# First two attentions of a two-block network: scaled negative queries, a minimum in the mask, rope on GpSimd, and an earlier copy

## The chip, the cores and the metric

The kernel runs on one core of a Trainium2 chip. What is measured is the device time of one execution, in microseconds; a run is one timed execution, and times are given as the median of several.

A core has five engines with queues of their own: TensorE (PE, matrix products and transposes, written to PSUM), VectorE (DVE), ScalarE (ACT), GpSimd (POOL), and SyncE (SP), which here only issues DMAs. Engines meet in semaphores: an instruction adds one to a semaphore when it is done, and another engine waits in its own queue until the count is there. An engine executes its queue strictly in order.

## The reference, cut to what matters

One batch of 256 tokens with model width 1024 goes through a first block and then two layers of a second one, all in fp32. The change lies wholly in the first block's mixer, which has two attentions over the same 256 tokens:

```python
h = rms_norm(x, mix_norm_g[layer])
proj = h @ w_in[layer]
q_a, k_a, v_a, c_q, c_kv, k_pe, gate_a, gate_b = jnp.split(proj, splits, axis=-1)
q_a = apply_rope(q_a.reshape(B, S, A_HEADS, A_HEAD_DIM), cos_a, sin_a)      # 8 heads of 64
k_a = apply_rope(k_a.reshape(B, S, A_HEADS, A_HEAD_DIM), cos_a, sin_a)
y_a = moba_attention(q_a, k_a, v_a)     # one block of 256 keys: plain causal attention here
# second attention (MLA), 8 heads of 64 + 32 with rope on the 32:
q = (rms_norm(c_q, q_norm_g) @ w_q_up).reshape(B, S, B_HEADS, B_NOPE + B_ROPE)
kv = (rms_norm(c_kv, kv_norm_g) @ w_kv_up).reshape(B, S, B_HEADS, B_NOPE + B_V)
# q_pe, k_pe: apply_rope; k_pe is shared by the heads
# both attentions, per head:
s = q @ k.T * scale ; s = where(k_pos <= q_pos, s, -inf) ; p = softmax(s) ; y = p @ v
merged = sigmoid(gate_a) * (y_a @ w_branch_a) + sigmoid(gate_b) * (y_b @ w_branch_b)
x = x + merged @ w_out[layer]
```

Here `apply_rope` gives, for the halves x1 and x2, `x1*cos - x2*sin` and `x2*cos + x1*sin`. Then come a product-key expert layer (128 x 128 experts, all computed densely in the kernel) and the second block.

## The kernel before, in words

All weights come as a stream of 128-row chunks of up to 1024 columns, in one fixed order (`chunk_plan`). The four-deep ring `w_raw` takes them. Each chunk j passes four hands: SP loads it (once the split of chunk j-4 is complete), ACT writes its rounded part w_hi (`split`, L1345; needs the load, and PE done with chunk j-4), POOL writes the rest w_lo = w_raw - w_hi (`rest`, L1863), and PE multiplies three products for each block (hi·hi, lo·hi, hi·lo; L625 to L627 for row groups, L818 to L820 in `gate_b`). ACT and POOL do this three chunks ahead of PE. Their other work is written by hand between these steps: ACT's `split_to(n)` runs the splits up to chunk n-1, and POOL's main loop has calls ahead of `rest(j)` for chosen j.

The order of groups in the stage that matters: qk (8 chunks), vc (8), ga (8), qup (2), kvup (1), gb (8), br_a (4), br_b (4), wout (8). In ga, PE also transposes the rotated queries and keys of the first attention (`a_maps`, ahead of chunk ga+2) and the normalised low-rank rows (`c_maps`, ahead of ga+6). ACT copies the former to QTA (L1423). ACT computes the sigmoid of gate a from the finished banks (L1381, `evacuate("ga", ...)`), and PE starts qup only when these banks are free.

Then one loop over 16 heads u runs: 0 to 7 are the first attention's, 8 to 15 the second's. For each, PE does in this order: `causal_fills(u)`, the three transposes of the probabilities (L756, waits for exponential u; for heads 5 to 12 it waits also for `qb_E`, since the PSUM bank mb is used by the b_map too, and for heads 13 and 14 for `yA_E`); `scores(u+2)` (L747, L748); `head_values(u-1)` (L762 to L764); for u from 4 to 11 `b_map(u)` (L789), the transposes of two heads of QB (even u) or KF (odd u); for u 12 and 13 `y_map` (L799), transposes of the first attention's result; and `gate_b(u)`, one sixteenth of the gate b product, two heads to a chunk, which is spread over the heads so that PE has work while the softmax is computed. `gate_b(0)` writes banks 2 and 3, and waits for `kv_act`: kvup's second half was there.

DVE does per head `masked` (L2198): scores plus mask out of PSUM to Sm with the row maximum (a custom instruction and an accumulator read for each half), and then L2203, which multiplies the 128x2 maxima by -scale, for the bias of the exponential. Behind it in the same iteration stands head-specific work: for u = 1 the first half of KF and VB (L2228, L2229), for u = 2 to 6 the rope of the second attention (L2238 to L2257: six instructions for the queries QB in place, six for the keys, two that copy the rotated keys into KF for all heads), for u = 10 the normalisation `branch_out(0)` (L2208, L2211), for u = 6 to 13 the copy of the transposed heads to QTB (L2264), for u = 14 and 15 the low part of yA (L2269).

ACT does per head the two exponentials with accumulated sums (L1453, L1455), then `copy_probs(u-1)` (L1435), then special work: at u = 1 the splits of gb+1 and gb+2, the copies of token half 1 of KF and VB (L1465, L1466) out of banks 2 and 3, which signal `kv_act`, and the split of gb+3; at odd u from 3 a split; at u = 8 the copy of gate b's first half (L1444); at u = 12 and 13 the high part of yA (L1477).

Of the kernel before, what the change touches and what calls it, by code (L numbers as in the profile page):

```python
# [194 lines left out]
def share(semaphore, signals):  # L195
# [33 lines left out]
    **share("small_dve", [("angles", 1), ("rope_a", 1), ("cn", 1), ("cT", 3), ("rope_q", 1),  # L229
                          ("rope_k", 1), ("rope_b", 2), ("y", 4), ("best", 1), ("picks", 1),  # L230
# [3 lines left out]
    **share("small_pool", [("l2_r", 1), ("vb", 1), ("zg", 1), ("v_mean", 1), ("kd", 1), ("v_r", 1),  # L234
# [6 lines left out]
def program(nc, ins, out):  # L241
    ctx = ExitStack()
    with ctx:
# [1084 lines left out]
        def _(act):  # L1328
# [118 lines left out]
            for u in range(A_H + B_H):  # L1447
                scale = (A_DH if u < A_H else B_DK) ** -0.5
                act.wait_ge(sem("masked"), u + 1)
                if u >= 2:  # L1450

                    act.wait_ge(sem("pT"), upto("pT", u - 1))
                f(Pr[:, u % 2, 0:P], Sm[:, u % 2, 0:P], ACT.Exp, bias=mx[:, u, 0:1], scale=scale,  # L1453
                  accum_out=sums[:, u, 0:1]).then_inc(sem("exp0"), 1)
                f(Pr[:, u % 2, P:3 * P], Sm[:, u % 2, P:3 * P], ACT.Exp, bias=mx[:, u, 1:2],  # L1455
                  scale=scale, accum_out=sums[:, u, 1:2]).then_inc(sem("exp"), 1)
                if u:
                    copy_probs(u, PT, "pT", "pv", u - 1, "pT_E")
                if u == 1:

                    split_to(FIRST["gb"] + 3)
                    for n in range(2):
# [367 lines left out]
        def _(pool):  # L1830
# [35 lines left out]
            def block_masks():  # L1866
# [6 lines left out]
                causal_mask(causal1)  # L1873
# [170 lines left out]
        def _(dve):  # L2044
# [172 lines left out]
            for u in range(A_H + B_H):  # L2217
                dve.wait_ge(sem("scores"), u + 1)
                if u >= 2:

                    dve.wait_ge(sem("exp"), u - 1)
                masked(Sm[:, u % 2, :], col[u % 2], causal, mx[:, u, :],
                       (A_DH if u < A_H else B_DK) ** -0.5, "masked")
# [7 lines left out]
                if u == 2:  # L2231
                    cos, sin = (over(ang[:, :, ph, 32:48], [P, NT, 8, 16], 2) for ph in (1, 0))
                    q1, q2 = QB[:, :, :, 64:80], QB[:, :, :, 80:96]
                    k1, k2 = VC[:, :, 896:912], VC[:, :, 912:928]
                    rq = [rope_t[:, :, 8 * a:8 * a + 8, 16 * b:16 * b + 16] for a in range(2)
                          for b in range(2)]
                    rk = [rope_u[:, :, a, 0:16] for a in range(6)]
                    go(v.tensor_tensor(rq[0], q1, cos, ALU.mult))  # L2238
                    go(v.tensor_tensor(rq[1], q2, sin, ALU.mult))
                if u == 3:  # L2240
                    go(v.tensor_tensor(rq[2], q2, cos, ALU.mult))
                    then(v.tensor_tensor(rq[3], q1, sin, ALU.mult))
                if u == 4:
                    go(v.tensor_tensor(q1, rq[0], rq[1], ALU.subtract))
                    then(v.tensor_tensor(q2, rq[2], rq[3], ALU.add), "rope_q")
                if u == 5:
                    kc, ks = ang[:, :, 1, 32:48], ang[:, :, 0, 32:48]
                    go(v.tensor_tensor(rk[0], k1, kc, ALU.mult))
                    go(v.tensor_tensor(rk[1], k2, ks, ALU.mult))
                    go(v.tensor_tensor(rk[2], k2, kc, ALU.mult))  # L2250
                    then(v.tensor_tensor(rk[3], k1, ks, ALU.mult))
                    go(v.tensor_tensor(rk[4], rk[0], rk[1], ALU.subtract))
                    then(v.tensor_tensor(rk[5], rk[2], rk[3], ALU.add), "rope_k")
                if u == 6:
                    dve.wait_ge(sem("dve"), counts["dve"])
                    for n in range(2):
                        then(v.tensor_copy(KF[:, :, :, 64 + 16 * n:80 + 16 * n],  # L2257
                                           over(rk[4 + n], [P, NT, 8, 16], 2)), "rope_b")
# [669 lines left out]
```

## Time and profile before

| what | value |
|---|---|
| three runs | 1779.05, 1779.22, 1781.5 us; median 1779.22 |
| the profiled execution, its time | 1778.86 us |
| its span (first to last instruction) | 1777.1 us |
| mean granted TensorE clock | 0.992 of full |
| busy: PE / ACT / DVE / POOL | 97% / 52% / 51% / 58% |
| HBM read | 285.01 MB, 162 GB/s mean over the span |

Time and span differ by 1.8 us outside the instructions. The profile comes from one execution. Its views are used here as follows: the first part gives each engine's share; the list of waits says who waited for whom; the timeline gives one engine's instructions in order with the idle time before each; windows give each engine's busy time and the granted clock in a stretch (1.00 is 2.4 GHz, 0.50 is 1.2 GHz). An idle time in brackets names the engine and line whose signal ended it, by the latest signal found. The ends of PE's matmuls are modelled.

### The profile page before, as it was taken

How to read it: one execution, taken by the hardware profiler on the slowest of the kernel's cores; microseconds unless marked ns; L12 is line 12 of the kernel's file. 1: busy time of each engine (PE TensorE's matmuls, PEld its weight loads, DVE VectorE, ACT ScalarE, POOL GpSimd, SP SyncE). 2: the span in 40 equal slices, each digit the busy share in tenths (PEclk: the TensorE clock that was granted, in tenths of full speed). 3: DMA queues.
4: the chain of work that ended last, by engine and by line, in shares of the span. 5: the costliest groups of instructions: out<-in, count | busy, mean ns of one | idle time of the engine just before them, and what ended most of it. 6: DMA issues, size and time to landing. Idle time of an engine off the chain costs nothing.

```text
span 1777.1 us, 32153 instructions
## 1 busy us (share of the span) xinstructions
PE 1728.1 (97%) x10852; PEld 1549.5 (87%) x10852; DVE 905.0 (51%) x1838; ACT 925.3 (52%) x1596; POOL 1037.8 (58%) x542
## 2 busy tenths in 40 slices
PE   8989999999999999999999999899999999999998
PEld 6778899999999999888888888888999877789997
DVE  6563329990777776555555547743111266521112
ACT  5555556676333334544544556625554566555544
POOL 7835768888666665000000057716888886588886
PEclk9999999999999999999999999999999999999999
DMA  6523555555444444555555555104555555255553
GB/s 205 173 91 111 174 183 178 178 182 186 152 138 139 141 143 162 193 191 196 192 191 195 197 181 175 64 25 139 187 188 186 177 171 165 69 188 187 188 185 123
DMA packets 83074, 288.23 MB, mean 162 GB/s; under 512 B 9264, under 2 KB 9264, under 8 KB 82480
## 3 DMA queue, kind: packets, MB, share of 16 engines
q1 hardware_dynamic: 82560, 286.10, 49.1%
q10 hardware_dynamic: 432, 1.05, 0.2%
q8 instruction: 50, 0.82, 0.2%
q14 instruction: 32, 0.26, 0.0%
HBM read 285.01 MB, written 2.10 MB: 162 GB/s over the span
## 4 chain that ended last, share of the span: by engine, by line
PE 90%; ACT 3%; DVE 3%; POOL 2%; issue 2%; DMA 0%; DVEq 0%; ACTq 0%; POOLq 0%
PE acc L625 14%; PE acc L626 14%; PE acc L627 14%; PE col L662 12%; PE col L663 12%; PE col L664 12%; PE mb L923 3%; POOL w_lo L1863 1%; PE acc L1074 1%; PE mb L697 1%; ACT hT_hi L1369 1%; ACT w_hi L1345 1%; PE acc L1197 0%; PE mb L904 0%; PE col L1074 0%
## 5 line engine op out<-in xcount | busy, mean ns | idle before, releaser
L1863 POOL TENSOR_TENSOR w_lo<-w_raw,w_hi 128x1024 fp32r<-128x1024 f32 (+1 forms) x410 | 975.6, 2400 | 351.3 <-ACT w_hi L1345 350.8
L1345 ACT ACTIVATE w_hi<-w_raw 128x1024 fp32r<-128x1024 f32 (+1 forms) x539 | 565.3, 1052 | 350.9 <-PE acc L627 305.4
L662 PE MATMUL col<-hT_hi,w_hi 128*128 128x256 f32 x1632 | 468.1, 287 | 2.1 <-DVE hT_lo L2080 1.5
L664 PE MATMUL col<-hT_hi,w_lo 128*128 128x256 f32 x1632 | 461.9, 283 | 0.0
L663 PE MATMUL col<-hT_lo,w_hi 128*128 128x256 f32 x1632 | 461.8, 283 | 0.0
L662 PEld LDWEIGHTS col<-hT_hi,w_hi 128*128 128x128 f32 x1632 | 312.7, 192 | 5.1 <-issue 1.9
L663 PEld LDWEIGHTS col<-hT_lo,w_hi 128*128 128x128 f32 x1632 | 312.9, 192 | 2.3
L664 PEld LDWEIGHTS col<-hT_hi,w_lo 128*128 128x128 f32 x1632 | 312.6, 192 | 0.0
L625 PE MATMUL acc<-w_hi,W_hi 128*128 128x512 f32 x512 | 199.3, 389 | 0.0
L626 PE MATMUL acc<-w_lo,W_hi 128*128 128x512 f32 x512 | 199.3, 389 | 0.0
L627 PE MATMUL acc<-w_hi,W_lo 128*128 128x512 f32 x512 | 199.3, 389 | 0.0
L1905 POOL TENSOR_SCALAR_AFFINE_SELECT WST<-WST 128x512 f32<-128x512 f32 x1 | 0.6, 635 | 320.3 <-DMA WST<-in_gmlp_w 320.3
L2687 DVE CAST H_hi<-mb 128x256 fp32r<-128x256 f32 x64 | 27.2, 424 | 289.4 <-ACT mb L1717 289.4
L2449 DVE TENSOR_TENSOR w_lo<-w_raw,w_hi 128x1024 fp32r<-128x1024 f32 x128 | 156.2, 1221 | 0.7 <-ACT w_hi L1345 0.6
L625 PE MATMUL acc<-w_hi,hT_hi 128*128 128x512 f32 x368 | 144.8, 394 | 9.0 <-POOL w_lo L1863 3.5
L626 PE MATMUL acc<-w_lo,hT_hi 128*128 128x512 f32 x368 | 142.6, 388 | 0.0
L627 PE MATMUL acc<-w_hi,hT_lo 128*128 128x512 f32 x368 | 142.0, 387 | 0.0
L2427 DVE TENSOR_TENSOR W_lo<-act_e,W_hi 128x256 fp32r<-128x256 f32 x128 | 54.5, 426 | 147.3 <-ACT W_hi L1554 146.7
L627 PEld LDWEIGHTS acc<-w_hi,W_lo 128*128 128x128 f32 x512 | 96.1, 188 | 20.0
L626 PEld LDWEIGHTS acc<-w_lo,W_hi 128*128 128x128 f32 x512 | 96.1, 188 | 19.9
L625 PEld LDWEIGHTS acc<-w_hi,W_hi 128*128 128x128 f32 x512 | 96.1, 188 | 19.8
L625 PE MATMUL acc<-w_hi,H_hi 128*128 128x512 f32 x256 | 100.4, 392 | 0.0
(543 smaller groups left out, 2681.6 us busy)
## 6 DMA issues: line engine op xcount, KB each, us to landing
w_raw<-in_expert_u SPq DMA_DIRECT2D x128, 512.0 KB, 3.5
w_raw<-in_expert_v SPq DMA_DIRECT2D x128, 512.0 KB, 3.5
w_raw<-in_w_mlp SPq DMA_DIRECT2D x128, 512.0 KB, 3.5
w_raw<-in_w_in SPq DMA_DIRECT2D x24, 512.0 KB, 3.7
w_raw<-in_w_qkv_o SPq DMA_DIRECT2D x24, 512.0 KB, 3.8
w_raw<-in_w_query SPq DMA_DIRECT2D x16, 512.0 KB, 3.7
w_raw<-in_w_gate SPq DMA_DIRECT2D x16, 512.0 KB, 3.5
w_raw<-in_w_qkv_e SPq DMA_DIRECT2D x12, 512.0 KB, 3.8
```

The lines of the kernel that those rows point to most:

```text
L625: mm(o, hi(t), w_hi[:, s, a:b], start=first, stop=False)
L626: mm(o, hi(t), w_lo[:, s, a:b], start=False, stop=False)
L627: m = mm(o, lo(t), w_hi[:, s, a:b], start=False, stop=last)
L662: mm(o, wh[:, k, :], hi[:, k, :], start=k == 0, stop=False)
L663: mm(o, wh[:, k, :], lo[:, k, :], start=False, stop=False)
L664: m = mm(o, wl[:, k, :], hi[:, k, :], start=False, stop=k == KD - 1)
L923: m = mm(mb[s % 2][:, t * P:(t + 1) * P], hot2[:, s % 2, t, :], hot1[:, s % 2, t, :], start=True, stop=True)
L1345: f(w_hi[:, s, 0:w], w_raw[:, s, 0:w], ACT.Copy).then_inc(sem(f"hi{s}"), 1)
L1863: g.tensor_tensor(w_lo[:, s, 0:w], w_raw[:, s, 0:w], w_hi[:, s, 0:w].bitcast(F32), ALU.subtract).then_inc(sem(f"lo{s}"), 1)
L2427: v.tensor_tensor(lo[:, q, :], act_e[:, c, :], hi[:, q, :].bitcast(F32), ALU.subtract).then_inc(sem("W_lo"), 1)
L2449: v.tensor_tensor(w_lo[:, s, :], w_raw[:, s, :], w_hi[:, s, :].bitcast(F32), ALU.subtract).then_inc(sem(f"lo{s}"), 1)
L2687: v.tensor_copy(H_hi[:, s, :], H_q[s]).then_inc(sem("H_hi"), 1)
```

## The change

The queries of both attentions carry -scale: ACT's copy of the transposed queries of the first attention to QTA multiplies them by -1/8, and DVE's copy to QTB of the second attention's transposed queries by -96^-0.5. The mask holds +1e30 in place of -1e30 above the diagonal, `masked` takes the minimum instead of the maximum, and the exponential has scale -1 with that minimum as its bias; the multiplication of L2203 falls away. The rope of the second attention moves from DVE to POOL: the keys' before `rest(ga+6)`, the queries' before `rest(gb+1)`. In ACT's iteration u = 1, the copies of KF and VB come right behind the exponentials, ahead of `copy_probs(0)` and ahead of the splits of gb+1 to gb+3.

```diff
@@ ACT
                 f(QTA[:, 2 * b:2 * b + 2, :].rearrange("p a s -> p (a s)"), mb[b % 2][:, :],
-                  ACT.Copy).then_inc(sem("qa_E"), 1)
+                  ACT.Copy, scale=-A_DH ** -0.5 if b < 2 else 1.0).then_inc(sem("qa_E"), 1)
...
             for u in range(A_H + B_H):
-                scale = (A_DH if u < A_H else B_DK) ** -0.5
...
-                f(Pr[:, u % 2, 0:P], Sm[:, u % 2, 0:P], ACT.Exp, bias=mx[:, u, 0:1], scale=scale,
+                f(Pr[:, u % 2, 0:P], Sm[:, u % 2, 0:P], ACT.Exp, bias=mx[:, u, 0:1], scale=-1.0,
                   accum_out=sums[:, u, 0:1]).then_inc(sem("exp0"), 1)
...
-                if u:
-                    copy_probs(u, PT, "pT", "pv", u - 1, "pT_E")
                 if u == 1:
-
-                    split_to(FIRST["gb"] + 3)
                     for n in range(2):
                         acc_full(act, "kvup", 2 + n)
                         kv = acc[2 + n][:, :].rearrange("p (h d) -> p h d", h=4)
                         f(KF[:, 1, 4 * n:4 * n + 4, 0:B_NOPE], kv[:, :, 0:B_NOPE], ACT.Copy)
                         f(VB[:, 1, 4 * n:4 * n + 4, :], kv[:, :, B_NOPE:], ACT.Copy).then_inc(
                             sem("kv_act"), 1)
+                if u:
+                    copy_probs(u, PT, "pT", "pv", u - 1, "pT_E")
+                if u == 1:
                     split_to(FIRST["gb"] + 4)
@@ POOL
-            def causal_mask(m):
+            def causal_mask(m, fill):
...
-            causal_mask(causal)
+            causal_mask(causal, -NEG)
...
+            def rotate_key():
+                pool.wait_ge(sem("ev_vc"), upto("ev_vc", 4))
+                pool.wait_ge(sem("rope_a"), upto("rope_a", 1))
+                x1, x2 = VC[:, :, 896:912], VC[:, :, 912:928]
+                rk = [rope_u[:, :, a, 0:16] for a in range(6)]
+                cos, sin = rope_cs()
+                g.tensor_tensor(rk[0], x1, cos, ALU.mult).then_inc(sem("rope_k"), 1)
+                g.tensor_tensor(rk[1], x2, sin, ALU.mult).then_inc(sem("rope_k"), 1)
+                g.tensor_tensor(rk[2], x2, cos, ALU.mult).then_inc(sem("rope_k"), 1)
+                g.tensor_tensor(rk[3], x1, sin, ALU.mult).then_inc(sem("rope_k"), 1)
+                pool.wait_ge(sem("rope_k"), 4)
+                g.tensor_tensor(rk[4], rk[0], rk[1], ALU.subtract).then_inc(sem("rope_k"), 1)
+                g.tensor_tensor(rk[5], rk[2], rk[3], ALU.add).then_inc(sem("rope_k"), 1)
+                pool.wait_ge(sem("rope_k"), 6)
+                for n in range(2):
+                    g.tensor_copy(KF[:, :, :, 64 + 16 * n:80 + 16 * n],
+                                  rk[4 + n].unsqueeze(2).to_broadcast([P, NT, 8, 16])).then_inc(
+                        sem("rope_b"), 1)
+            def rotate_queries():
+                pool.wait_ge(sem("ev_qup"), upto("ev_qup", 4))
+                x1, x2 = QB[:, :, :, 64:80], QB[:, :, :, 80:96]
...
+                g.tensor_tensor(rq[0], x1, cos, ALU.mult).then_inc(sem("rope_p"), 1)
+                g.tensor_tensor(rq[1], x2, sin, ALU.mult).then_inc(sem("rope_p"), 1)
+                g.tensor_tensor(rq[2], x2, cos, ALU.mult).then_inc(sem("rope_p"), 1)
+                g.tensor_tensor(rq[3], x1, sin, ALU.mult).then_inc(sem("rope_p"), 1)
+                pool.wait_ge(sem("rope_p"), 4)
+                g.tensor_tensor(x1, rq[0], rq[1], ALU.subtract).then_inc(sem("rope_p"), 1)
+                pool.wait_ge(sem("rope_p"), 5)
+                g.tensor_tensor(x2, rq[2], rq[3], ALU.add).then_inc(sem("rope_q"), 1)
...
+                if j == FIRST["ga"] + 6:
+                    rotate_key()
+                if j == FIRST["gb"] + 1:
+                    rotate_queries()
@@ DVE
-            def masked(dst, src, mask, top, scale, name):
+            def masked(dst, src, mask, low, name):
                 for t, (a, b) in enumerate(((0, P), (P, 3 * P))):
-                    i = v.tensor_tensor_reduce(dst[:, a:b], src[:, a:b], mask[:, a:b], 1.0, LOWEST,
-                                               ALU.add, ALU.max, top[:, t:t + 1])
-                    if t == 0:
-                        go(i)
-                then(i)
-                then(v.tensor_scalar(top, top, -scale, None, ALU.mult), name)
+                    i = v.tensor_tensor_reduce(dst[:, a:b], src[:, a:b], mask[:, a:b], 1.0, -LOWEST,
+                                               ALU.add, ALU.min, low[:, t:t + 1])
+                i.then_inc(sem(name), 1)
...
-                if u == 2:
-                    (the rope of u = 2 to 6: 12 tensor_tensor and 2 tensor_copy)
...
-                    then(v.tensor_copy(QTB[0:B_DK, 2 * b:2 * b + 2, :].rearrange("p a s -> p (a s)"),
-                                       mb[(u + 1) % 2][0:B_DK, :]), "qb_E")
+                    heads_ = QTB[0:B_DK, 2 * b:2 * b + 2, :].rearrange("p a s -> p (a s)")
+                    turned_ = mb[(u + 1) % 2][0:B_DK, :]
+                    if b < 4:
+                        then(v.tensor_scalar(heads_, turned_, -B_DK ** -0.5, None, ALU.mult), "qb_E")
+                    else:
+                        then(v.tensor_copy(heads_, turned_), "qb_E")
```

## Rows read from the trace of the kernel before

**Rows 1.** The page's first part: busy time, share of the span, instructions, by engine.
```profile
PE 1728.1 (97%) x10852; PEld 1549.5 (87%) x10852; DVE 905.0 (51%) x1838; ACT 925.3 (52%) x1596; POOL 1037.8 (58%) x542
```

**Rows 2.** The list of waits, 50 to 160 us: total us, times, longest.
```profile
PE mb L756 <- ACT Pr L1455: 4.2, 4, 1.9
```

**Rows 3.** Timeline of PE: start, duration, instruction, idle time before it and releaser.
```profile
76.94 0.48 PE L625 MATMUL acc<-w_hi,hT_hi 128*128 128x512 f32 x1
...
95.48 0.50 PE L818 MATMUL acc<-w_hi,hT_hi 128*128 128x512 f32 x1 [2.71 <-ACT VB L1466]
...
100.40 0.49 PE L756 MATMUL mb<-ident,Pr 128*128 128x128 f32 x3
...
102.36 0.48 PE L818 MATMUL acc<-w_hi,hT_hi 128*128 128x512 f32 x1
...
113.19 0.52 PE L756 MATMUL mb<-ident,Pr 128*128 128x128 f32 x3 [1.94 <-ACT Pr L1455]
...
130.19 0.52 PE L756 MATMUL mb<-ident,Pr 128*128 128x128 f32 x3 [1.12 <-ACT Pr L1455]
...
148.85 0.52 PE L756 MATMUL mb<-ident,Pr 128*128 128x128 f32 x3 [0.94 <-ACT Pr L1455]
```

**Rows 4.** Windows: stretch, length, busy of PE, PEld, DVE, ACT, POOL; clock, DMA, GB/s.
```profile
114.40:116.50 2.10, 2.10 (x11) 1.98 (x11) 0.81 (x5) 0.93 (x4) 0.00 (x0) 0.52 0.09 31
116.50:118.00 1.50, 1.50 (x6) 1.23 (x5) 0.69 (x1) 0.06 (x1) 0.00 (x0) 0.53 0.00 0
```

**Rows 5.** Timeline of ACT.
```profile
80.02 1.06 ACT L1345 ACTIVATE w_hi<-w_raw 128x1024 fp32r<-128x1024 f32 x1 [2.55 <-PE acc L627]
...
91.95 0.49 ACT L1435 ACTIVATE PT<-mb 128x384 f32<-128x384 f32 x1 [0.40 <-PE mb L756]
92.34 1.99 ACT L1345 ACTIVATE w_hi<-w_raw 128x1024 fp32r<-128x1024 f32 x2
...
125.00 1.38 ACT L1444 ACTIVATE GB<-acc,rstd 128x512 f32<-128x512 f32 x2 [1.92 <-PE acc L820]
...
147.44 0.50 ACT L1455 ACTIVATE Pr<-Sm,mx 128x256 f32<-128x256 f32 x1
```

**Rows 6.** Timeline of DVE.
```profile
79.16 0.49 DVE L2070 TENSOR_SCALAR cT_hi<-mb,cols 128x256 fp32r<-128x256 f32 x1
...
109.42 2.30 DVE L2203 TENSOR_SCALAR mx<-mx 128x2 f32<-128x2 f32 x1
...
112.40 0.69 DVE L2264 COPY QTB<-mb 96x512 f32<-96x512 f32 x1
...
146.18 1.85 DVE L2203 TENSOR_SCALAR mx<-mx 128x2 f32<-128x2 f32 x1
```

**Rows 7.** One line's instructions: duration in ns min/median/max, first and last start.
```profile
L2203 DVE TENSOR_SCALAR mx<-mx x16: 168/170/2297, 89.5 to 146.2; 128x2 f32<-128x2 f32 x16
```

**Rows 8.** Timeline of POOL.
```profile
67.28 4.78 POOL L1863 TENSOR_TENSOR w_lo<-w_raw,w_hi 128x1024 fp32r<-128x1024 f32 x2 [0.31 <-ACT w_hi L1345]
...
77.55 1.85 POOL L1863 TENSOR_TENSOR w_lo<-w_raw,w_hi 128x768 fp32r<-128x768 f32 x1 [0.88 <-ACT w_hi L1345]
...
85.84 2.38 POOL L1863 TENSOR_TENSOR w_lo<-w_raw,w_hi 128x1024 fp32r<-128x1024 f32 x1 [2.31 <-ACT w_hi L1345]
93.46 7.22 POOL L1863 TENSOR_TENSOR w_lo<-w_raw,w_hi 128x1024 fp32r<-128x1024 f32 x3 [5.23 <-ACT w_hi L1345]
```

**Rows 9.** Groups by form, DVE: count | busy us, mean ns | idle before.
```profile
L2780 DVE CUSTOM_DVE_ANT_0 S<-col,ALIBI 128x256 f32<-128x256 f32 x16 | 6.7, 419 | 0.0
```

**Rows 10.** Groups by form, POOL.
```profile
L1863 POOL TENSOR_TENSOR w_lo<-w_raw,w_hi 128x1024 fp32r<-128x1024 f32 x395 | 943.1, 2407 | 350.3 <-ACT w_hi L1345 349.9 <-issue 0.2
...
L1917 POOL TENSOR_TENSOR ms<-ss 128x1 f32<-128x1 f32 x18 | 4.6, 253 | 20.7 <-ACT junk L1361 20.7
...
L1899 POOL TENSOR_TENSOR masks<-masks 128x128 f32<-128x128 f32 x1 | 1.3, 1314 | 0.1
```

**Rows 11.** DMA issues, 71 to 77 us: KB each, us from issue to landing.
```profile
w_raw<-in_w_kv_up SPq DMA_DIRECT2D x1, 512.0 KB, 3.4
```

More of the change, by code:

```diff
@@ L228 @@
                           ("lam_exp", 1), ("qk_root", 2), ("o1_ss", 4)]),
[L229 to L230 removed]
+    **share("small_dve", [("angles", 1), ("rope_a", 1), ("cn", 1), ("cT", 3), ("y", 4), ("best", 1), ("picks", 1),
                           ("x_final", 4), ("sp", 2), ("g_ready", 1), ("k_map", 1),
@@ L233 @@
                           ("o1", 4)]),
-    **share("small_pool", [("l2_r", 1), ("vb", 1), ("zg", 1), ("v_mean", 1), ("kd", 1), ("v_r", 1),
+    **share("small_pool", [("rope_b", 2), ("rope_q", 1), ("l2_r", 1), ("vb", 1), ("zg", 1), ("v_mean", 1), ("kd", 1), ("v_r", 1),
                            ("gv", 1), ("dec_q", 1), ("o_r", 2),
@@ L1452, in _ @@
                     act.wait_ge(sem("pT"), upto("pT", u - 1))
-                f(Pr[:, u % 2, 0:P], Sm[:, u % 2, 0:P], ACT.Exp, bias=mx[:, u, 0:1], scale=scale,
+                f(Pr[:, u % 2, 0:P], Sm[:, u % 2, 0:P], ACT.Exp, bias=mx[:, u, 0:1], scale=-1.0,
                   accum_out=sums[:, u, 0:1]).then_inc(sem("exp0"), 1)
                 f(Pr[:, u % 2, P:3 * P], Sm[:, u % 2, P:3 * P], ACT.Exp, bias=mx[:, u, 1:2],
-                  scale=scale, accum_out=sums[:, u, 1:2]).then_inc(sem("exp"), 1)
-                if u:
-                    copy_probs(u, PT, "pT", "pv", u - 1, "pT_E")
+                  scale=-1.0, accum_out=sums[:, u, 1:2]).then_inc(sem("exp"), 1)
                 if u == 1:
-                    split_to(FIRST["gb"] + 3)
                     for n in range(2):
@@ L1848, in causal_mask @@
                     d = m[:, c * P:(c + 1) * P]
-                    then(g.affine_select(out=d, in_=d, compare_op=ALU.is_ge, fill=NEG, base=0,
+                    then(g.affine_select(out=d, in_=d, compare_op=ALU.is_ge, fill=fill, base=0,
                                          pattern=[[-1, P]], channel_multiplier=1), "causal")
-            causal_mask(causal)
+            causal_mask(causal, -NEG)
             g.iota(iota_row[:, :], [[1, P]], base=0, channel_multiplier=0,
@@ L1871, in block_masks @@
                 used(pool, V0 + 1)
-                causal_mask(causal1)
+                causal_mask(causal1, NEG)
                 for c, base in ((0, 0), (1, P), (2, 0)):
@@ L1921, in row_rstd, with rope_cs @@
                 norms[0] += 1
+            def rope_cs(heads_=None):
+                cs = [ang[:, :, ph, 32:48] for ph in (1, 0)]
+                return cs if heads_ is None else [c.unsqueeze(2).to_broadcast([P, NT, heads_, 16])
+                                                  for c in cs]
+            def rotate_key():
[16 more added lines that the diff above has]
+                        sem("rope_b"), 1)
@@ new lines, in rotate_queries @@
+            def rotate_queries():
+                pool.wait_ge(sem("ev_qup"), upto("ev_qup", 4))
+                x1, x2 = QB[:, :, :, 64:80], QB[:, :, :, 80:96]
+                rq = [rope_t[:, :, 8 * a:8 * a + 8, 16 * b:16 * b + 16] for a in range(2)
+                      for b in range(2)]
+                cos, sin = rope_cs(8)
+                g.tensor_tensor(rq[0], x1, cos, ALU.mult).then_inc(sem("rope_p"), 1)
[6 more added lines that the diff above has]
+                g.tensor_tensor(x2, rq[2], rq[3], ALU.add).then_inc(sem("rope_q"), 1)
@@ L2221, in _ @@
                     dve.wait_ge(sem("exp"), u - 1)
-                masked(Sm[:, u % 2, :], col[u % 2], causal, mx[:, u, :],
-                       (A_DH if u < A_H else B_DK) ** -0.5, "masked")
+                masked(Sm[:, u % 2, :], col[u % 2], causal, mx[:, u, :], "masked")
                 if u == 1:
@@ L2230, in _ @@
                              "ev_kvup")
-                if u == 2:
[L2232 to L2258, printed above, removed]
                 if u == A_H + 2:
```

## The prediction, made before the changed kernel was run

> **What bounds the kernel now.** First the page's first part: TensorE (PE) is busy for 97% of the span, so only time in which PE waits, or runs at the lower clock, can be won [rows 1]. The changed code runs between 57 and 155 us. There the list of waits has one wait of PE that comes four times, on the exponentials of L1455, 4.2 us in all [rows 2]. PE's own timeline shows where PE is idle: 2.71 us before 95.48, 1.94 before 113.19, 1.12 before 130.19, 0.94 before 148.85 (the fourth wait on L1455 is the small rest, before 144.26) [rows 3]. Between them PE works back to back: from the first gate step (95.48) to the third (102.36) two heads pass in 6.88 us, 3.44 a head. Last the windows: from 114.4 to 118.0 us, behind the wait of 1.94, the granted clock was 0.52 and 0.53, so nearly all at the lower level (1.2 GHz) [rows 4].
>
> A wait for several semaphores is put down to the last one that the profile names, so each needs its real cause.
> - Before 95.48 PE stands at the first gate step, which waits for `kv_act`, ACT's copies of KF and VB out of banks 2 and 3. ACT was done with the second exponential at 91.55 (91.95 less 0.40 idle), copied head 0's transposes, ran two splits (92.34 to 94.33), and only then those copies [rows 5]. PE had been ready at 92.77.
> - Before 113.19 the transposes of head 5 also wait for `qb_E`, the copy to QTB. It ended at 113.09, and stands in DVE's order behind the KF copies and L2203, a tensor_scalar on 128x2 numbers that took 2.30 us here [rows 6], where its median is 0.17 [rows 7]. All its operands lie in SBUF, and POOL was in a w_lo subtraction, as it was in three of them from 93.46 on, 2.41 us each [rows 8]: DVE stood until POOL's instruction was over.
> - Before 130.19 it is again that copy, this time behind the normalisation of the first attention, which stays.
> - Before 148.85 it is `yA_E`: the subtraction of L2269 stood behind another held L2203, from 146.18 to 148.03 [rows 6].
>
> **The change part by part.** The sum is made against the profiled execution, 1778.86 us, of which 1777.1 are span. The median of the runs, 1779.22, lies 0.36 above it.
>
> 1. *KF and VB ahead of the splits.* ACT can begin at 91.55. Before, the four copies lay between 94.33 and PE's start at 95.48, so they take 1.1; `kv_act` comes at 92.7 and PE is ready at 92.77. The wait of 2.71 goes. What is late next: copy_probs(0), 0.49, and three splits of 0.99 now stand behind the copies [rows 5], to 96.2, and exponential 2 behind them, about 0.9 long, to 97.1. PE reaches the transposes of head 2 4.92 us behind the first gate step (95.48 to 100.40), now at 97.7. Cover 0.6 us. Bounds -2.7, and -1.6 if exponential and copies both come 1.2 late. I take **-2.7**, since each duration is one of this stage.
> 2. *L2203 gone, the mask as a minimum.* The 16 instructions leave DVE, not PE's path. The minimum form runs already in the last attention, 419 ns for 128x256 [rows 9], as the maximum does here: no cost. In head 6 nothing stands before the QTB copy any more. It starts when PE's transposes are there and fits inside the gate step that follows them (3.44 less 1.96, the time from 100.40 to 102.36: 1.48): 0.69 for the plain copy, and scaled between 0.69 and 0.98 (twice the 0.49 of a tensor_scalar out of PSUM on 128x256 [rows 6]); I take 0.75. The wait goes: **-1.9**. So does what lay behind it: 2.10 x 0.48 + 1.50 x 0.47 = 1.7 us lost at half clock [rows 4]. Bounds 0, if the clock falls elsewhere, and -1.7; **-1.7**, as no such gap is left ahead of it.
> 3. *The wait before 130.19* shrinks by L2203's 0.17 and grows by the 0.06 of the scaled copy: **-0.1**.
> 4. *The wait before 148.85.* The subtraction then waits only for ACT's yA_hi, and the exponential of head 14 decides, whose last part ended at 148.0 (147.44 and 0.50) [rows 5]: **-0.8**, bounds 0 and -0.94.
> 5. *The scale in QTA.* The nearest ACT row with a scale, out of PSUM at 128x512, is 0.69 each (125.00) [rows 5], about 0.1 over the plain copy. Bounds 0 and +0.2, as two copies are scaled; I take 0: that scale was a tensor, this is a constant.
> 6. *rotate_key on POOL*, ahead of the subtraction of chunk ga+6: six instructions of 128x32, two of 128x256. POOL's rows are 253 ns at one element and 2407 at 1024 [rows 10], so 2.1 ns an element: 6 x 0.32 + 2 x 0.79 = 3.5 us. From below 8 x 0.253 = 2.0; from above 8 x 1.314 = 10.5, by the slowest such row (128x128). That subtraction is the second of the pair that ended at 72.06 [rows 8], and PE needs it at 76.94 [rows 3]: cover 4.9 us. SP issues the load of kvup when this subtraction ends; it lands 3.4 us later [rows 11], now at 79.0, and ACT's split of it started at 80.02 [rows 5]: cover 1.0 beyond the 3.5, and POOL is idle again by 77.55. **0**. Above 4.6 us the split is late, with it the sigmoid behind it on ACT, and PE, which waits for the sigmoid ahead of qup.
> 7. *rotate_queries on POOL*, ahead of gb+1: free at 88.22, POOL had nothing until 93.46 [rows 8]. Six of 128x256 at 0.79 and three waits: 5.0 us, to 93.3. From below 6 x 0.253 = 1.5; from above 6 x 2.63 = 15.8, at 1314 ns for each 128 elements. The subtraction of gb+1 follows ACT's split (94.2) and ends at 96.6; PE asks for it at the third gate step, 92.77 + 6.88 = 99.65. So the rotation may take 8.8 us, 1.4 an instruction. **0**.
> 8. *The rope instructions leave DVE.* PE waited for none of them; nothing more.
>
> A rule speaks against parts 6 and 7. POOL's row is 2407 ns for 128x1024 [rows 10], DVE's for 256 elements out of PSUM 0.49 [rows 6]. The Trainium skill, GPSIMD Engine Reference, section 4.1 Engine selection, gives elementwise work with two inputs to VectorE, because GpSimd is roughly 2x slower. By that, an estimate, the queries' six would take 2 x 0.49 each, 5.9 us in place of 5.0. Either lies inside the 8.8, so the sum would be the same; what the rule prices is the engine's time, not the path.
>
> Another bears on the scaled QTB copy. The tensor_scalar out of PSUM at 79.16 took 0.49 us [rows 6] beside a subtraction on POOL (77.55 to 79.40) [rows 8]: not held. The Trainium skill, SBUF — State Buffer, section Who interferes with whom, names tensor_scalar among the operations that may take the port pair that VectorE shares with GpSimd, given their operands. If it did here, each of the four scaled copies could cost up to 2.4; the row says it does not.
>
> Sum: 2.7 + 1.9 + 1.7 + 0.1 + 0.8 = 7.2. The later stages start on PE's work and on loads that PE's progress sets free, so it is carried to the end. 1778.86 - 7.2 = 1771.7 for an execution like the profiled one, and 1779.2 - 7.2 = 1772.0 for the median.
>
> **The rivals.**
> - *A new wait at heads 2 and 3.* ACT's queue is now copies, copy_probs, three splits, exponential; 1 us more in it and PE waits at head 2, and the clock may fall behind that gap. For it: a cover of only 0.6. Against: no step of ACT got longer. It takes 1.2 of part 1 and the 1.7 of the clock: 1774.9.
> - *The wait before 113.19 stays*, because something else than QTB held it. For it: the profile names the exponential. Against: that one too stood behind L2203, and 113.09 fits 113.19. Then 1.9 and 1.7 are missing: 1775.6.
> - *GpSimd is slow on small, strided, broadcast operands* (the other side). At the 1314 ns row's rate rotate_key takes 10.5, and PE waits for ga+6 until 69.7 + 10.5 + 2.4 = 82.6 instead of 76.94: +5.7. rotate_queries ends at 104.2 and gb+1 at 106.6 instead of 99.65: +7.0. The clock adds 1.7 at least. -7.2 + 14.4 = +7.2: 1786.4. It costs from 1.3 times my price on (the 4.6 of part 6) and from 1.8 times in part 7; at 2.2 times the two cost 3.1 and 2.2 and the clock 1.7, about what the change gains: slower from there. Against: it is one row, the two others give a sixth of it for one element and half of it an element for many.
> - *Nothing measurable*: GpSimd at 1.7 to 2.1 times my price, or a later stage that waits on something not set free by PE: 1777.
>
> **How the numbers follow.** A difference under 0.2%, 3.6 us, can't be told from none for this kernel. Forecast 0.70; new wait 0.11; the wait stays 0.06; nothing measurable 0.09; slow GpSimd 0.04. Over 3.6 us faster: the forecast, and 0.13 of the first two rivals' 0.17: 0.83. Within: 0.13. Slower: 0.04. The forecast's own range is 1770.3 to 1773.7. The range goes down by 2.4 for a clock that also stays up elsewhere, and up over the first two rivals: 1769.6 to 1775.8.
>
> **What would show it.** Right: the first gate step at about 92.8 with no idle before it; none before head 5's transposes, and a granted clock of 1.00 from 92 to 128; about 1 us of idle left before head 9's and 0.15 before head 14's transposes; POOL's rope at 69.7 to 73.2 and 88.4 to 93.4, each instruction under 0.9 us. Wrong: any of them over 1.4 us, PE waiting for w_lo at ga+6 or the third gate step, a longer wait ahead of qup, or a stretch at the lower clock before 155.

## The result: 10 to 12 us faster, where 7.2 were forecast

| kernel | median us (executions) | range | ratio to before, 95% interval |
|---|---|---|---|
| before, first comparison | 1780.36 (4) | 1779.05 to 1783.83 | |
| changed, first comparison | 1770.11 (4) | 1769.12 to 1771.48 | 0.9938 (0.9919 to 0.9958) |
| before, second comparison | 1781.48 (23) | 1776.79 to 1787.78 | |
| changed, second comparison | 1769.75 (6) | 1769.06 to 1770.98 | 0.9931 (0.9915 to 0.9948) |

The change is faster, as forecast, but by 0.6 to 0.7% instead of 0.4%. The medians themselves, 1770.11 and 1769.75, lie inside the range of 1769.6 to 1775.8 us. As ratios to 1779.22 that range is 0.9946 to 0.9981, and both measured ratios lie below it. The difference is in the kernel before, which is slower than its first three runs showed (1779.22): its executions spread over 11 us, those of the changed kernel over 2.4. The two profiled executions, by contrast, differ by what was forecast: spans 1777.1 and 1769.7, 7.4 us.

The experiments below were timed in three groups, each with the kernel before beside it: medians 1781.48 (23 executions), 1781.53 (20) and 1781.17 (23). Ratios are to the kernel before of the same group. The changed kernel was timed again only in the first, so a difference from it can be one between groups. One execution of rope_on_dve, 2125.17 us at a mean clock of 0.751 where its others had 0.994 to 0.995, is left out.

PE's timeline of the changed kernel (L755 is the old L756, L817 the old L818, L624 the old L625):

```profile
92.77 0.50 PE L817 MATMUL acc<-w_hi,hT_hi 128*128 128x512 f32 x1
...
97.69 0.49 PE L755 MATMUL mb<-ident,Pr 128*128 128x128 f32 x3
...
99.65 0.48 PE L817 MATMUL acc<-w_hi,hT_hi 128*128 128x512 f32 x1
...
108.36 0.49 PE L755 MATMUL mb<-ident,Pr 128*128 128x128 f32 x3
...
123.38 0.52 PE L755 MATMUL mb<-ident,Pr 128*128 128x128 f32 x3 [0.77 <-ACT Pr L1454]
...
141.28 0.55 PE L755 MATMUL mb<-ident,Pr 128*128 128x128 f32 x3 [0.17 <-ACT Pr L1454]
...
147.19 0.47 PE L624 MATMUL acc<-w_hi,yA_hi 128*128 128x512 f32 x1 [0.21 <-issue]
```

Held against [rows 3]: the first gate step has no idle time before it, nor have head 2's transposes (97.69) nor head 5's (108.36). 1.12 us before head 9's became 0.77, 0.94 before head 14's 0.17. The stage ends, with the start of br_a, at 147.19 instead of 154.63.

The clock in the stretch in which it had fallen before [rows 4], a window of the changed kernel (length; busy PE, PEld, DVE, ACT, POOL; clock; DMA; GB/s):

```profile
92.00:128.00 36.00, 35.23 (x215) 28.83 (x215) 12.11 (x49) 23.12 (x63) 17.41 (x9) 1.00 0.35 103
```

ACT, to hold against [rows 5]: copies first, then copy_probs, then three splits, and exponential 2 from 95.61 to 96.50, so done 1.2 us before PE needs it at 97.69:

```profile
91.34 0.36 ACT L1460 ACTIVATE KF<-acc 128x256 f32<-128x256 f32 x1
...
92.13 0.37 ACT L1461 ACTIVATE VB<-acc 128x256 f32<-128x256 f32 x1
92.40 0.49 ACT L1435 ACTIVATE PT<-mb 128x384 f32<-128x384 f32 x1
92.77 2.96 ACT L1344 ACTIVATE w_hi<-w_raw 128x1024 fp32r<-128x1024 f32 x3
95.61 0.40 ACT L1452 ACTIVATE Pr<-Sm,mx 128x128 f32<-128x128 f32 x1
...
95.99 0.51 ACT L1454 ACTIVATE Pr<-Sm,mx 128x256 f32<-128x256 f32 x1
```

POOL, to hold against [rows 8]. A 128x32 product starts every 0.21 us, a 128x256 one every 0.70, and the two copies take 0.75 together. The last line is a subtraction during which DVE makes the copy shown next:

```profile
69.75 0.25 POOL L1934 TENSOR_TENSOR rope_u<-VC,ang 128x32 f32<-128x32 f32 x1
...
71.24 0.75 POOL L1943 COPY KF<-rope_u 128x256 f32<-128x256 f32 x2
...
88.53 0.73 POOL L1954 TENSOR_TENSOR rope_t<-QB,ang 128x256 f32<-128x256 f32 x1 [0.21 <-DVE QB L2154]
...
92.25 0.73 POOL L1961 TENSOR_TENSOR QB<-rope_t 128x256 f32<-128x256 f32 x1
93.91 9.38 POOL L1861 TENSOR_TENSOR w_lo<-w_raw,w_hi 128x1024 fp32r<-128x1024 f32 x4 [0.93 <-ACT w_hi L1344]
...
106.60 2.39 POOL L1861 TENSOR_TENSOR w_lo<-w_raw,w_hi 128x1024 fp32r<-128x1024 f32 x1 [3.31 <-ACT w_hi L1344]
```

DVE in head 6, to hold against [rows 6]; the scaled copy lasts as long as the plain one (0.69), although POOL's subtraction of 106.60 to 108.99 runs beside it:

```profile
107.18 0.69 DVE L2279 TENSOR_SCALAR QTB<-mb 96x512 f32<-96x512 f32 x1 [0.60 <-PE mb L788]
```

### The profile page after: what moved, and what is told of

It is laid out like the page before. It is cut to its first block, busy times and chain, and to the rows that moved or that the text cites. A ratio compares the mean times of both kernels' runs of the same rounds, so it can differ in the third digit from the quotient of the medians.

```text
span 1769.7 us, 32125 instructions
## 1 busy us (share of the span) xinstructions
PE 1726.9 (98%) x10852; PEld 1548.3 (87%) x10852; DVE 888.5 (50%) x1808; ACT 925.4 (52%) x1596; POOL 1044.8 (59%) x556
## 4 chain that ended last, share of the span: by engine, by line
PE 90%; ACT 3%; DVE 3%; POOL 2%; issue 1%; DMA 0%; DVEq 0%; ACTq 0%; POOLq 0%
PE acc L624 14%; PE acc L625 14%; PE acc L626 14%; PE col L661 12%; PE col L662 12%; PE col L663 12%; PE mb L922 3%; POOL w_lo L1861 1%; PE acc L1073 1%; PE mb L696 1%; ACT hT_hi L1368 1%; PE col L1073 0%; ACT w_hi L1344 0%; PE acc L1196 0%; PE mb L903 0%
## 5 line engine op out<-in xcount | busy, mean ns | idle before, releaser
L624 PE MATMUL acc<-w_hi,W_hi 128*128 128x512 f32 x512 | 199.2, 389 | 0.0
L625 PE MATMUL acc<-w_lo,W_hi 128*128 128x512 f32 x512 | 199.2, 389 | 0.0
L624 PE MATMUL acc<-w_hi,hT_hi 128*128 128x512 f32 x368 | 144.9, 394 | 8.9 <-POOL w_lo L1861 3.6
L625 PE MATMUL acc<-w_lo,hT_hi 128*128 128x512 f32 x368 | 142.6, 387 | 0.0
L624 PEld LDWEIGHTS acc<-w_hi,W_hi 128*128 128x128 f32 x512 | 96.1, 188 | 20.0
L625 PEld LDWEIGHTS acc<-w_lo,W_hi 128*128 128x128 f32 x512 | 96.1, 188 | 19.9
L624 PE MATMUL acc<-w_hi,H_hi 128*128 128x512 f32 x256 | 100.4, 392 | 0.0
```

The lines of the kernel that those rows point to most:

```text
L624: mm(o, hi(t), w_hi[:, s, a:b], start=first, stop=False)
L625: mm(o, hi(t), w_lo[:, s, a:b], start=False, stop=False)
```

## The experiments

**Where the 11 us are: the stage or outside it.** The changed kernel again, and two more profiled executions of the kernel before, unchanged, called a and b here.

> The changed kernel once more. Every stage boundary of its trace lies 7.4 to 7.5 us ahead of the kernel before, from the start of br_a (147.19 instead of 154.63) to the end. Theory A, the change gives exactly its stage's 7.4 us: ratio 0.9958, difference of medians 7 to 8. Theory B, something outside the stage gives 3 us more: ratio 0.9938 again, about 11. Under A the larger difference came from executions of the kernel before in which the stretches at the lower TensorE clock (1186, 1206, 1504 and 1528 us) lasted longer.

> One more look at the kernel before. If its time is over 1781, clock theory: its trace has a stretch at the lower clock right behind the first gate step (94 to 105 us), which the profiled execution of 1778.86 us had not; if its time is under 1779, none. Rival: the excess lies in the stretches around 1186, 1206, 1504 and 1528 us.

> The same once more, for a second execution: over 1781 with the clock low behind the first gate step, or under 1779 without. Rival as for the first.

after_again gave 1769.75 us. The size is that of theory B (11.7 us by the medians, ratio 0.9931), its place is not: the table below shows nothing outside the stage that would give it. Executions a and b took 1784.06 and 1779.71 us. The first agrees with the forecast. The second had no fall behind the first gate step either, but lies between the two bounds that I had set (1779 and 1781). PE's timeline of execution a:

```profile
95.42 0.80 PE L818 MATMUL acc<-w_hi,hT_hi 128*128 128x512 f32 x1 [2.71 <-ACT VB L1466]
...
117.46 0.52 PE L756 MATMUL mb<-ident,Pr 128*128 128x128 f32 x3 [1.95 <-ACT Pr L1455]
...
129.28 0.52 PE L756 MATMUL mb<-ident,Pr 128*128 128x128 f32 x3 [1.21 <-issue]
...
161.87 0.47 PE L625 MATMUL acc<-w_hi,yA_hi 128*128 128x512 f32 x1 [0.21 <-issue]
```

and its windows:

```profile
88.00:94.00 6.00, 4.70 (x27) 3.25 (x23) 4.76 (x20) 3.98 (x11) 0.80 (x2) 1.00 0.29 87
94.00:96.00 2.00, 0.58 (x1) 0.50 (x2) 1.97 (x2) 2.00 (x6) 2.00 (x2) 0.66 0.00 0
96.00:104.00 8.00, 8.00 (x24) 6.00 (x23) 6.34 (x9) 2.65 (x10) 4.58 (x2) 0.50 0.71 197
104.00:106.00 2.00, 2.00 (x10) 1.22 (x8) 0.00 (x0) 0.78 (x2) 0.00 (x0) 0.78 0.00 0
...
117.00:119.00 2.00, 1.54 (x8) 0.91 (x8) 0.36 (x1) 0.49 (x2) 0.00 (x0) 0.89 0.74 260
119.00:125.00 6.00, 6.00 (x22) 5.28 (x23) 1.50 (x6) 1.44 (x6) 0.00 (x0) 0.50 0.01 3
```

The clock fell towards the end of the 2.71 us wait (1.00 before 94, 0.66 from 94 to 96) and stayed at the lower level until about 105 (L818 takes 0.80 instead of 0.50), and again behind the wait of 1.95 for longer than in the first trace. There is also a new wait, 1.21 before head 7's transposes. DVE's timeline shows why: with PE later, masked(8) and the next subtraction on POOL (126.06 to 128.44) meet, and L2203 is held there too:

```profile
126.46 2.00 DVE L2203 TENSOR_SCALAR mx<-mx 128x2 f32<-128x2 f32 x1
128.49 0.69 DVE L2264 COPY QTB<-mb 96x512 f32<-96x512 f32 x1
```

Execution b had only the second fall, again longer, and the same new wait (1.09 before 124.87, with L2203 held for 1.89 from 122.16):

```profile
113.00:115.00 2.00, 1.83 (x10) 1.33 (x10) 0.37 (x4) 0.49 (x1) 0.00 (x0) 0.84 0.66 229
115.00:121.00 6.00, 6.00 (x22) 5.19 (x22) 1.20 (x4) 1.86 (x6) 0.00 (x0) 0.50 0.00 0
```

Every profiled execution, split at the start of br_a (first PE instruction that reads yA_hi):

| profiled execution | span | stage's end | rest |
|---|---|---|---|
| before, first | 1777.1 | 154.63 | 1622.5 |
| before, b | 1778.0 | 157.45 | 1620.6 |
| before, a | 1782.3 | 161.87 | 1620.4 |
| changed | 1769.7 | 147.19 | 1622.5 |
| changed again | 1767.9 | 147.13 | 1620.8 |
| without_kv | 1773.0 | 150.09 | 1622.9 |
| kv_only | 1773.0 | 151.22 | 1621.8 |
| min_only | 1774.3 | 153.31 | 1621.0 |
| rope_only | 1779.1 | 158.39 | 1620.7 |
| pe_filled | 1778.8 | 157.60 | 1621.2 |
| rope_on_dve | 1769.9 | 146.99 | 1622.9 |
| two_more | 1768.2 | 145.95 | 1622.3 |
| slow_key | 1772.4 | 151.16 | 1621.2 |
| slow_queries | 1776.9 | 155.91 | 1621.0 |

The rest varies by 2.5 us whatever the kernel (the later stretches at the lower clock, around 1180, 1200, 1500 and 1525 us, are longer or shorter). The kernel before reaches the end of this stage at three times that lie 7.2 us apart, the changed kernel in both traces at the same to 0.06. So in the executions that were traced the difference is made in the stage, and the rival, the later stretches, isn't what made execution a slow. Executions of over 1784.06 us were not traced.

The mean clock of every execution says that the spread is one of the clock, though not in which stretch: of the 23 of the kernel before in the second comparison, the five at 0.994 took 1776.8 to 1778.6 us, the five at 0.989 or 0.990 took 1785.2 to 1787.8. A mean clock lower by 0.005 over 1777 us is 8.9 us. The ten of the changed kernel had 0.994 to 0.996.

**ACT's order alone, and the change without it.** kv_only is the kernel before with the u == 1 lines of ACT as changed; without_kv the changed kernel with the old ones:

```diff
-                if u:
-                    copy_probs(u, PT, "pT", "pv", u - 1, "pT_E")
                 if u == 1:
-                    split_to(FIRST["gb"] + 3)
                     (the copies of KF and VB)
+                if u:
+                    copy_probs(u, PT, "pT", "pv", u - 1, "pT_E")
+                if u == 1:
                     split_to(FIRST["gb"] + 4)
```

> The kernel before with only the copies of KF and VB ahead of copy_probs and the splits. Mine: the first gate step starts at 92.8 instead of 95.48 and the wait ahead of head 5's transposes stays near 1.9 us, so -2.8 us. Rival (ACT's order only moves the wait): PE waits at heads 2 to 4 instead, under -1.5. The clock falls behind the wait at head 5 as before, or not; then 1.7 more.

> The changed kernel with ACT's old order in head 1 (splits of gb+1 and gb+2 ahead of the copies of KF and VB). The wait of 2.7 us before the first gate step comes back. Clock theory: behind that wait the granted clock falls to the lower level in part of the executions, for about 11 us as in the trace with the rope alone moved (94 to 105), and that costs up to 5.5 us; so the median is 6 to 9 us over the changed kernel's, and the times spread over 5 us or more. Rival, the wait costs only its length: +2.8, times within 2 us of each other as those of the changed kernel are, and the rest of the 11 us lies elsewhere.

kv_only: 1773.57 us (1771.75 to 1774.77), ratio 0.9949 (0.9932 to 0.9966): 7.9 us by the medians, where 2.8 were forecast and the wait it removes is 2.7 long. without_kv: 1775.71 us (1772.41 to 1778.67), ratio 0.9974 (0.9963 to 0.9984), 6.0 over the changed kernel, with a spread of 6.3: the low end of what the clock theory gave, and twice the rival's 2.8. In its own profiled execution the wait was there (2.72 before 95.67) and the clock did not fall behind it; that execution ended the stage 2.9 late. Its slowest two, 1778.6 and 1778.7 us, had a mean clock of 0.991, its fastest 0.995. So this wait costs about 2.8 in one traced execution and 6.0 in the median; that the clock falls right behind it in the slower ones of without_kv is argued from execution a, not traced.

The forecast for kv_only missed the waits as well. Head 5 waited for nothing (the KF copies ran at 108.35, before POOL's subtraction of 108.96), and head 4 had a new wait. Exponential 4 waited for masked(4), which stood on DVE behind two rope products of the queries, 128x256 with both inputs in SBUF. They took 2.57 and 2.58 us instead of 0.42 beside two subtractions on POOL:

```profile
105.94 0.55 PE L756 MATMUL mb<-ident,Pr 128*128 128x128 f32 x3 [1.38 <-ACT Pr L1455]
```
```profile
98.90 2.57 DVE L2240 TENSOR_TENSOR rope_t<-QB,ang 128x256 f32<-128x256 f32 x1
101.40 2.58 DVE L2241 TENSOR_TENSOR rope_t<-QB,ang 128x256 f32<-128x256 f32 x1
```
```profile
98.80 4.89 POOL L1862 TENSOR_TENSOR w_lo<-w_raw,w_hi 128x1024 fp32r<-128x1024 f32 x2
```

The clock fell behind that wait:

```profile
108.00:110.00 2.00, 2.00 (x10) 1.69 (x10) 1.56 (x6) 1.76 (x5) 1.04 (x1) 0.52 0.00 0
110.00:112.00 2.00, 2.00 (x8) 1.44 (x7) 0.00 (x0) 0.08 (x1) 1.34 (x1) 0.62 0.04 8
```

Much of the 7.9 is therefore not the clock behind the first wait. Execution b had no such fall, and still ended the stage 6.2 us later than kv_only: 2.7 for the wait itself, 0.6 for a shorter second wait (1.38 for 1.95), 1.1 for the wait at head 7 that is gone, and 1.7 for a shorter fall (1.7 us lost instead of 3.4). An earlier PE meets POOL's subtractions at other places.

**PE kept busy in that wait.** pe_filled is the kernel before with

```diff
                 if u == 0:
+                    chunk_in(j)
+                    for n in range(11):
+                        mm(mb[1][:, :], hT_hi[:, 0, 0:P], w_hi[:, s, 0:512], start=True, stop=True)
                     pe.wait_ge(sem("kv_act"), 2)
```

> The kernel before, with 11 products of 128x128 by 128x512 (0.23 us each, 2.5 us) put on PE into a bank that is not in use, in the place of the wait before the first gate step. Nothing else changes: that step still starts at 95.5. Clock theory: the granted clock no longer falls behind it, so the slower executions go: median 1778 to 1779, none over 1781. Rival, the spread comes from elsewhere (the later stretches at the lower clock): median 1781.5 and times up to 1787 as before.

1779.76 us (1774.04 to 1783.99), ratio 0.9991 (0.9979 to 1.0004): the forecast was missed. The median lies over its 1778 to 1779, three of twelve executions took over 1781, and the kernel is not told apart from before. The fill did its work in the trace, no idle time is left before the first gate step and the clock was up there. But the wait of head 5 followed, the clock fell behind it from about 114 to 121, and the held L2203 of head 8 (L2206 here) cost head 7 another 1.46:

```profile
112.94 0.52 PE L756 MATMUL mb<-ident,Pr 128*128 128x128 f32 x3 [1.96 <-ACT Pr L1458]
...
125.02 0.52 PE L756 MATMUL mb<-ident,Pr 128*128 128x128 f32 x3 [1.46 <-issue]
```

So the spread does not come from the first wait alone; the fall behind the second and what follows it are part of it. Whether the fill moved the first fall onto the second wait, these runs can't say.

**The rope alone.** rope_only is the kernel before with the POOL functions, their calls and the shares of the semaphores added, and DVE's rope removed.

> The kernel before with only the rope of the second attention on GpSimd; L2203's multiplication, the maximum and ACT's order stay. If L2203, held by POOL, is what holds QTB at head 6: the wait at head 5 stays at about 1.2 (the two KF copies are gone, 0.7 us), the first gate step stays at 95.5: -0.7, and -2.4 if the clock then stays up. If the rope instructions on DVE were the cause: the wait goes, -3.6.

1780.04 us (1775.0 to 1782.31), ratio 0.9985 (0.9972 to 0.9998). Head 5 waited 1.31, as L2203 alone would have it, and the first gate step 2.97; behind both the clock fell. PE's and DVE's timelines:

```profile
95.48 0.79 PE L817 MATMUL acc<-w_hi,hT_hi 128*128 128x512 f32 x1 [2.97 <-ACT VB L1465]
...
116.95 0.52 PE L755 MATMUL mb<-ident,Pr 128*128 128x128 f32 x3 [1.31 <-issue]
```

```profile
113.84 2.30 DVE L2248 TENSOR_SCALAR mx<-mx 128x2 f32<-128x2 f32 x1
116.17 0.69 DVE L2281 COPY QTB<-mb 96x512 f32<-96x512 f32 x1
```

**The minimum alone, and all but the rope.** min_only has scaled queries, the minimum and no L2203, with rope on DVE and ACT's old order; rope_on_dve is the same with ACT's new order.

> The kernel before with only the scaled queries, the minimum and no L2203; rope stays on DVE, ACT's order stays. Theory of the prediction, L2203 is the cause at head 5: the wait goes, with it the clock's fall, and 0.8 at head 14: -4.5. Rival: the KF copies of head 6 also lie wholly in SBUF and are held in L2203's place by the same subtraction on POOL: wait at head 5 stays at 1.8, only head 14's 0.8 and 0.1 at head 9: -0.9.

> The changed kernel with the rope put back on DVE in heads 2 to 6; scaled queries, minimum and ACT's new order stay. If L2203 was the whole cause at head 5, this is as fast as the changed kernel (-7.4 against before). If the KF copies are held in its place, the wait at head 5 returns (1.9) and with it perhaps the clock's fall (1.7): -3.6 to -5.5.

min_only: 1779.44 us (1776.02 to 1784.96), ratio 0.9991 (0.9978 to 1.0005). The rival held: a wait at head 5 stayed (1.57, forecast 1.8), and the kernel can't be told from before. PE at head 5, then DVE and POOL in head 6:

```profile
112.84 0.52 PE L756 MATMUL mb<-ident,Pr 128*128 128x128 f32 x3 [1.57 <-issue]
```

```profile
109.33 2.68 DVE L2253 COPY KF<-rope_u 128x256 f32<-128x256 f32 x2
112.05 0.69 DVE L2263 TENSOR_SCALAR QTB<-mb 96x512 f32<-96x512 f32 x1
```
```profile
109.34 2.52 POOL L1863 TENSOR_TENSOR w_lo<-w_raw,w_hi 128x1024 fp32r<-128x1024 f32 x1 [4.22 <-ACT w_hi L1345]
```

With L2203 gone the KF copies, also wholly in SBUF, are held by the same subtraction, PE waits 1.57, and its clock falls (0.72 mean from 112 to 118). Taking away L2203 without the KF copies, or the KF copies without L2203, leaves most of the wait. Both together, which is without_kv, leave none and are 5.5 us faster than before by the medians, where min_only alone is 2.0 and rope_only alone 1.4.

rope_on_dve: 1770.94 us (1769.37 to 1771.67), ratio 0.9943 (0.9926 to 0.9961), so 1.2 over the changed kernel by the medians. There the KF copies ran at 106.40, unheld in 0.62, because POOL's subtraction came only at 107.27. With ACT's new order the two happen not to meet; my 3.6 to 5.5 was wrong, since I had put POOL where it was before. So once the rest is changed, moving the rope is worth 1.2 us or less in these runs.

**How slow GpSimd may be.** slow_queries adds 16 products of 128x256 into the scratch, slow_key 20 of 128x32:

```diff
                 pool.wait_ge(sem("rope_p"), 4)
+                for n in range(16):
+                    g.tensor_tensor(rq[n % 4], (x1, x2, x2, x1)[n % 4], (cos, sin)[n % 2],
+                                    ALU.mult).then_inc(sem("rope_p"), 1)
+                    if n % 4 == 3:
+                        pool.wait_ge(sem("rope_p"), n + 5)
                 g.tensor_tensor(x1, rq[0], rq[1], ALU.subtract).then_inc(sem("rope_p"), 1)
-                pool.wait_ge(sem("rope_p"), 5)
+                pool.wait_ge(sem("rope_p"), 21)
...
                 pool.wait_ge(sem("rope_k"), 4)
+                for n in range(20):
+                    g.tensor_tensor(rk[n % 4], (x1, x2, x2, x1)[n % 4], (cos, sin)[n % 2],
+                                    ALU.mult).then_inc(sem("rope_x"), 1)
+                    if n % 4 == 3:
+                        pool.wait_ge(sem("rope_x"), n + 1)
```

> The changed kernel with 16 more products of 128x256 in rotate_queries on GpSimd (results the same): 0.70 each, 11.2 us, so the rotation ends at 104.2 instead of 92.98, which is what the rival of a slow GpSimd priced. By the prediction's cover of 8.8 us: w_lo of gb+1 at 106.6, PE asks for it at 99.65, waits 6.9 us, the clock falls behind it (1.7): about +1.2 against before, +8.6 against the changed kernel. If the cover is larger than that (POOL's subtraction not what PE waits for): under +6 against the changed kernel.

> The changed kernel with 20 more products of 128x32 in rotate_key: 0.21 each and five waits, 4.7 us, 6.9 in all instead of 2.2. By the prediction's chain (cover 4.6 to the load of kvup and ACT's split, 4.9 to PE's need of ga+6): ga+6 2.0 us late for PE, kvup's split 2.3 late, with the sigmoid and qup behind it: 2 to 2.5 us slower than the changed kernel. If the covers are larger: no difference.

slow_queries: 1779.75 us (1777.88 to 1783.04), ratio 0.9993 (0.9981 to 1.0005), 10.0 over the changed kernel, 8.6 forecast. In its trace the stage ended at 155.91, 8.7 later than in the changed kernel's. Its third gate step:

```profile
106.78 0.76 PE L817 MATMUL acc<-w_hi,hT_hi 128*128 128x512 f32 x1 [7.10 <-POOL w_lo L1861]
```

slow_key: 1773.56 us (1770.25 to 1775.13), ratio 0.9955 (0.9940 to 0.9970), 3.8 over, 2 to 2.5 forecast. PE waited 2.00 for w_lo of ga+6, and the stage ended at 151.16, 4.0 later; the clock stood at 0.72 in the mean from 79 to 85. Both covers of the prediction are real, and in both the wait was sized rightly. In slow_key the clock behind it, 1.7 us, had been left out of the forecast. In slow_queries it was 1.7 in the trace, as forecast; why the median is 1.3 us more is not shown.

**Two more orders.**

```diff
-            split_to(FIRST["qup"] + 3)
+            split_to(FIRST["qup"] + 2)
             evacuate("ga", halves(GA), ACT.Sigmoid, "ev_ga", R_START)
...
-                if u == A_H + 2:
-                    branch_out(0)
                 if 6 <= u <= 13:
                     (the QTB copy)
+                if u == A_H + 2:
+                    branch_out(0)
```

> The changed kernel with two orders changed: DVE's normalisation of the first attention (head 10) behind the QTB copy instead of ahead of it, and ACT's split of kvup behind the sigmoid of gate a instead of ahead of it. Mine: the 0.77 us idle before head 9's transposes goes, about 0.2 comes back at the values of head 8, and the 0.58 before qup goes: -1.2 against the changed kernel, first gate step at 92.2. Rival: the split of kvup comes late and PE waits for kvup: 0 or slower.

1769.22 us (1767.88 to 1770.22), ratio to before 0.9935 (0.9920 to 0.9951). In the trace both waits went as said (0.17 left before qup, 0.23 at the values of head 8), and the stage ended at 145.95, 1.2 us ahead of the changed kernel. The medians differ by 0.5, too little to call it faster by the runs.

## Why the prediction was right in its steps and wrong in its size

The step that failed is the price of the clock. For the profiled execution the sum was right: 1771.7 us forecast, 1771.48 measured. But it took one fall, 1.7 us, from one trace and carried it to the median. The kernel before loses more than that in other executions, and there a further wait comes with it.

- *Part 1*, KF and VB ahead: right to the hundredth in the trace (first gate step 92.77, third 99.65; head 2's transposes 97.69), with more cover than I had worked out (1.2 us for 0.6). Its price was wrong. It gave the wait its length, 2.7, and nothing for the clock, since in the one trace the clock had not fallen behind it. Of the six traces with this wait unfilled, two had the fall (execution a and rope_only), four had not (before, b, without_kv, min_only). Execution a lost about 4.7 us by it (0.5 x 8.0 from 96 to 104, 0.44 from 104 to 106, 0.3 for the 0.58 us of work before 96). It also had no price for where an earlier PE meets POOL's subtractions, which was worth 3.4 us more between execution b and kv_only.
- *Part 2* failed in the term "1.7 us lost at half clock ... bounds 0 and -1.7". That upper bound was the size of one fall in one execution. The seven traces with a wait at head 4 or 5 all had a fall behind it: about 1.7 us in before, kv_only, min_only and rope_only, about 3.4 in a, b and pe_filled (b: 0.3 + 3.0 + 0.1). In the latter three comes a follow-up that the prediction did not have: PE meets POOL anew, and L2203 is held a second time, with 1.1 to 1.5 us of wait at head 7. That the QTB copy stood behind L2203 and the KF copies is borne out by min_only and rope_only; the text leaned on L2203, and min_only shows the KF copies would have taken its place. With ACT's old order, only moving the rope and dropping L2203 together took the wait away.
- The sum for execution b: idle time 8.0 there against 1.1 in the changed kernel, 6.9, and 3.4 of clock: 10.3, where the stage ends 10.26 later. The prediction had 5.5 and 1.7 for these two. For execution a 7.0 and 8.1: 15.1, against 14.7.
- *Parts 3 and 4*: 0.35 and 0.77 for 0.1 and 0.8. The scaled QTB copy costs nothing; it was 0.69, not 0.75.
- *Part 5*: no cost; the idle time at the second pair of transposes of QTA stayed 0.25.
- *Parts 6 and 7*: 2.2 us for 3.5, and 4.5 for 5.0. The 128x256 copy, which I priced as a product, costs half of one. In the slow rival the two rows set against the 1314 ns one were misread: 253 is a fifth of it, not a sixth, and 2407 for 1024 elements is 2.35 ns an element against 10.3, under a quarter, not half. Neither enters the sum.
- The range failed with the clock: it allowed 2.4 us "for a clock that also stays up elsewhere", while this stage alone varies by 7.2. And it was counted from a median of three executions that lay 2.3 us under that of 23; that part was the luck of a small sample.

None of the rivals came true in the changed kernel; the slow GpSimd's part for the queries was priced nearly rightly, as slow_queries shows. What stays open is how the falls are spread over the executions that were not traced, and why the clock fell behind the same wait in some executions and not in others.

## What to carry to other kernels

When PE waits a few microseconds in mid-stream, price the wait as its length plus a fall of the clock, with a chance, even if the one trace at hand shows no fall behind it; a second wait in the same trace that does show one is the warning. Time the kernel before often enough to see its spread: three executions showed 2.5 us, no more than four of the changed kernel (2.4), and 23 showed 11. And when DVE's instructions are held by one on POOL, the wait goes only when every instruction in the chain that can be held has gone, moved or no longer meets it: taking one away hands the wait to the next.

## What the runs showed of the hardware

- The same wait, 2.71 us long to 0.01, was followed by a granted clock of 1.00 in one execution and of 0.50 from 96 to 104 us in another of the same program.
- The length of the wait alone did not decide whether the clock fell. Waits of 1.31 to 1.96 us at head 4 or 5 had a fall behind them in all seven traces that have one; waits of 1.09 to 1.46 us at head 7 had none in three.
- Beside a subtraction on POOL, three kinds of DVE instruction wholly in SBUF were held alike: a copy took 2.4 us instead of 0.3 (min_only: 2.68 for two, 0.62 unheld), a tensor_scalar on 128x2 numbers 2.3 instead of 0.17, a product with two inputs 2.6 instead of 0.42 (kv_only). DVE's tensor_scalar out of PSUM to SBUF was not held in the changed kernel (107.18, beside 106.60 to 108.99) and took as long as the plain copy (0.69 at 96x512).
- POOL's small products took 0.21 us from start to start at 32 elements and 0.70 at 256, and a copy of 256 with a broadcast source 0.37. Between the first two lie 2.2 ns an element, so by an estimate from these two 0.14 us is the instruction's own: most of a product of 32 elements, a fifth of one of 256.
